# Expert weights relaid by partition, loaded in a half and two quarters (in) and in halves (out), with one quarter going through a buffer of its own

## The chip, the cores and the metric

The kernel runs on one core of one Trainium2 chip. The metric is device time in microseconds (us) of that core, for one launch. The comparisons are between medians of runs on the same chip.

## The reference, cut to what matters

Two transformer blocks on 256 tokens of width 1024, all in float32. The first block (gated attention and retention mixer, convolutional feed-forward) and the mixer of the second block come first; the end of the second block is a mixture of 32 experts, and that is where the change is:

```python
logits = (t @ w_router + b_router)            # 256 tokens, 32 experts
top_val, top_idx = lax.top_k(logits, 4)       # each token goes to 4 experts
gate_w = jax.nn.softmax(top_val, axis=-1)
...
hb = xb @ w_exp_in[e] + b_exp_in[e]           # xb: the tokens of expert e; w_exp_in[e]: 1024 x 2048
g = jnp.minimum(hb[:, :1024], 7.0)
u = jnp.clip(hb[:, 1024:], -7.0, 7.0)
a = g * jax.nn.sigmoid(1.702 * g) * (u + 1.0)
y = a @ w_exp_out[e] + b_exp_out[e]           # w_exp_out[e]: 1024 x 1024
...
h = layer_norm(ALPHA * h + sum over the 4 experts of gate_w * y)
```

One expert has 8 MB of in-weights and 4 MB of out-weights, read once: 32 experts are about 403 MB (12.58 million bytes each), out of 494 MB that the whole kernel moves.

## The kernel before, in words

**Tiling of an expert.** The contraction over 1024 goes in 8 steps k of 128 rows. `win` holds the in-weights of one expert (8 steps of 128 x 2048), `wout` its out-weights (8 steps of 128 x 1024). Both lie in `big_mem` and there is one of each: a step's place is free for the next expert once TensorE has used it. The tokens of an expert are gathered by matmuls with a 0/1 matrix (`gather`, L1038) into `xT`. They are worked in groups of 32, 64, or 64 and 32 rows, by how many tokens the expert has (`GROUPS`); an expert with more than 64 tokens has two groups, 96 rows together.

**One expert on TensorE** (`one_pass`): `gu` (L1055) adds up 8 steps of in-weights, counting `gu_part` after each step; then gathers for the next expert, transposes for the way back (L1077) and of the activations (L1085); then `second` (L1097) adds up 8 steps of out-weights, counting `y_part`; then `combine` (L1111, L1120) adds the result to the tokens' rows in PSUM, and the next expert's `gu` begins. VectorE (L2320 to L2332) and ScalarE (L1706, L1713, L1717, L1722) do the activation and the copies out of PSUM between these.

**The loads** are all issued by SyncE (SP) onto one queue, in program order. Before: four quarters of `win` (2 MB each, two steps) and four of `wout` (1 MB each). Each DMA waits until TensorE has used the two steps it overwrites, and SP goes through its waits in order. TensorE waits for a quarter before the first step that it covers. In DRAM the rows are taken so that partition p has rows 2p and 2p+1 of a 256-row piece; so the gather and the transpose take every second column (a stride of 2 in `h1` and `moe["a"]`).

**Order.** Experts 0 and 1 come first, then the others in an order that VectorE works out from the token counts (`order`, L2352), which spaces the large ones out.

**Before the experts** the DMA queue carries the dense weights through a ring of three slots (`load`, L393), each load waiting for its slot. The in-weights of expert 0 are issued at L460, its out-weights at L463, those of the later experts at L477 and L480.

Of the kernel before, what the change touches and what calls it, by code (L numbers as in the profile page):

```python
# [7 lines left out]
F32 = mybir.dt.float32  # L8
# [5 lines left out]
ACT = mybir.ActivationFunctionType  # L14
# [89 lines left out]
x0_in x1_in tab_stay_in tab1_in cols_in small_in router_in tab2_in rows_in rows_out toep_in toep_ps toep_ready ln12_in bias_in  # L104
slot0_in slot1_in slot2_in up0_in up1_in
own_act own_dve square_ready root_ready
# [17 lines left out]
def program(nc, ins, out):  # L124
# [3 lines left out]
    with ExitStack() as ctx:  # L128
        s = {n: ctx.enter_context(nc.semaphore(n)) for n in EVENTS}
        win_in = [ctx.enter_context(nc.semaphore(f"win{k}_in")) for k in range(KD // 2)]  # L130
        wout_in = [ctx.enter_context(nc.semaphore(f"wout{k}_in")) for k in range(KD // 2)]


        ring_mem = ctx.enter_context(nc.sbuf_tensor("ring_mem", [P, 3 * 4096], F32))
# [248 lines left out]
        wout_x = ins["w_exp_out_2"].rearrange("l e (k p j) n -> (l e) k p j n", p=P, j=2)  # L383


        @block.sync
        def _(sp):
# [70 lines left out]
            sp.wait_ge(s["merged_ready"], KD)  # L458
            for k in range(KD // 2):
                sp.dma_start(win[:, 2 * k:2 * k + 2, :], win_x[0, k]).then_inc(win_in[k], 16)  # L460
            sp.wait_ge(s["out_ps"], T)
            for k in range(KD // 2):
                sp.dma_start(wout[:, 2 * k:2 * k + 2, :], wout_x[0, k]).then_inc(wout_in[k], 16)  # L463

            sp.wait_ge(s["counts_ready"], 1)
            done = sp.alloc_register("sp_done")
            sp.reg_mov(done, 0)

            def expert(before, cur):
# [5 lines left out]
                for k in range(KD // 2):  # L475
                    sp.wait_ge(s["gu_part"], KD * others + 2 + 2 * k)
                    sp.dma_start(win[:, 2 * k:2 * k + 2, :], win_x[cur, k]).then_inc(win_in[k], 16)  # L477
                for k in range(KD // 2):
                    sp.wait_ge(s["y_part"], KD * others + 2 + 2 * k)
                    sp.dma_start(wout[:, 2 * k:2 * k + 2, :], wout_x[cur, k]).then_inc(wout_in[k], 16)  # L480

            expert(slice(0, 1), 1)
            sp.wait_ge(s["order_ready"], 1)
            with sp.Fori(2, E) as e:
                before = sp.value_load(order[0:1, bass.ds(e - 1, 1)], min_val=0, max_val=E - 1)
                expert(bass.ds(before, 1), sp.value_load(order[0:1, bass.ds(e, 1)], min_val=0, max_val=E - 1))
            for t in range(T):
# [61 lines left out]
        def _(pe):  # L549
# [483 lines left out]
            def gather(lo, hi, bank=7):  # L1033

                for k in range(lo, hi):
                    c = SLOTS * (k % EARLY)
                    for t in range(T):
                        last = mm(ps[:, bank, c:c + SLOTS], h1[:, t, SEQ * (k // 2) + k % 2:SEQ * (k // 2 + 1):2], moe["picks"][:, t, :], start=(t == 0), stop=(t == T - 1))  # L1038
                if hi in (EARLY, KD):
                    last.then_inc(s["gather_ps"], 1)  # L1040
# [6 lines left out]
            def gu(blocks, landed_all, tokens_all):  # L1047
# [15 lines left out]
                for k in range(KD):  # L1063
                    if k == EARLY:
                        pe.wait_ge(s["xT_ready"], tokens_all)
                    if k % 2 == 0:
                        pe.wait_ge(win_in[k // 2], landed_all)
# [12 lines left out]
            def turn_a(at, m):  # L1080

                w = D * m // P
                for c in range(w // P):
                    place = ps[:, 5, P * c:P * (c + 1)] if m > XS else ps[:, 4 + at // XS, SEQ + P * c:SEQ + P * (c + 1)]
                    last = nc.tensor.transpose(place, moe["a"][:, KD * at + SEQ * (c // 2) + c % 2:KD * at + SEQ * (c // 2 + 1):2], ident)  # L1085
                last.then_inc(s["aT_ps"], 1)

            def second(blocks, landed_all):

                for k in range(KD):  # L1090
                    if k % 2 == 0:
                        pe.wait_ge(wout_in[k // 2], landed_all)
                    for b, (at, m) in in_turn(blocks, k):
# [33 lines left out]
            for t in range(T):  # L1127
                if t == 0:
                    pe.wait_ge(s["pick0_ready"], 1)
                else:  # L1130
                    pe.wait_ge(s["picks_ready"], 1)
                    pe.wait_ge(s["h1_ready"], T)
                for k in range(KD):
                    c = SLOTS * (k % EARLY)
                    last = mm(ps[:, 7 if k < EARLY else 6, c:c + SLOTS], h1[:, t, SEQ * (k // 2) + k % 2:SEQ * (k // 2 + 1):2], moe["picks"][:, t, :],
                              start=(t == 0 and k in (0, EARLY)), stop=(t == T - 1), skip_group_check=True)
                    if t == T - 1 and k in (EARLY - 1, KD - 1):
                        last.then_inc(s["gather_ps"], 1)
# [99 lines left out]
        def _(act):  # L1238
# [518 lines left out]
            with act.Fori(0, E) as e:  # L1757
# [5 lines left out]
                with act.If(extra > 0):  # L1763
                    with act.If(extra < 2):
                        one_pass(GROUPS[1])
                    with act.If(extra > 1):
# [4 lines left out]
                        act.nop()  # L1771
                    act.nop()
                act.nop()
                act.wait_ge(s["order_ready"], 1)
# [673 lines left out]
```

## Time and profile before

| | us |
|---|---|
| median of 3 runs (1468.63 to 1469.0) | 1468.64 |
| the profiled execution: its own time | 1468.93 |
| its span, first to last instruction | 1467.1 |
| TensorE busy (share of the span) | 1314.9 (90%) |
| VectorE busy | 464.9 (32%) |
| ScalarE busy | 390.4 (27%) |
| GpSimd busy | 221.7 (15%) |
| longest shares of the chain that ended last | DMA of in-weights 25%, TensorE L1055 16%, TensorE L1097 7% |

The page of the profile has the busy time of each engine, a strip of 40 slices over the span, the chain of waits that ended last, the costliest groups of instructions, and the DMA issues with the time until they landed. A matmul's busy time says when the array had work, not how well it was used. Where an engine was idle, the view names what ended the idle time. The experts take the last 25 of the 40 slices.

### The profile page before, as it was taken

What the parts mean: (1) busy time and instruction counts of PE and PEld (TensorE: products, weight loads), DVE (VectorE), ACT (ScalarE), POOL (GpSimd) and SP (SyncE); (2) the same over time, 40 slices, a digit from 0 to 9 for tenths busy, and PEclk for the clock granted to TensorE, in tenths of its full rate; (3) what the DMA queues carried; (4) which work ended last, traced back from release to release, by engine and by line L of the source; (5) the groups of instructions that cost most, each with busy time, mean ns of one, the idle gap of its engine ahead of it and who ended that gap; (6) DMA issues with size and microseconds to landing.
All of it is one profiled execution on the core that took longest, in us unless ns stands there. A gap on an engine that the chain in (4) does not pass through costs nothing.

```text
span 1467.1 us, 25925 instructions
## 1 busy us (share of the span) xinstructions
PE 1314.9 (90%) x9475; PEld 819.1 (56%) x9476; DVE 464.9 (32%) x916; ACT 390.4 (27%) x728; POOL 221.7 (15%) x129
## 2 busy tenths in 40 slices
PE   7999999999999997887899888988889988998886
PEld 7787999878999853343334433443433434343333
DVE  2756777664534961111102110211111101110112
ACT  5556666555657420000001000110010001000101
POOL 6772122007774300000000000000000000000000
PEclk9999999999999999999999999999999999999998
DMA  9432667755443789999999999999999999999996
GB/s 329 170 113 58 181 185 234 287 193 178 167 173 116 269 334 421 425 429 424 425 426 428 427 426 424 427 427 427 424 428 427 421 424 428 427 426 424 428 426 273
DMA packets 114537, 494.40 MB, mean 337 GB/s; under 512 B 7633, under 2 KB 57153, under 8 KB 81505
## 3 DMA queue, kind: packets, MB, share of 16 engines
q1 hardware_dynamic: 113011, 491.50, 83.4%
q10 hardware_dynamic: 1486, 2.34, 0.5%
q8 instruction: 28, 0.46, 0.1%
q14 instruction: 12, 0.10, 0.0%
HBM read 492.76 MB, written 1.06 MB: 337 GB/s over the span
## 4 chain that ended last, share of the span: by engine, by line
PE 59%; DMA 29%; DVE 5%; issue 3%; ACT 3%; POOL 1%; SPq 0%; DVEq 0%; ACTq 0%; POOLq 0%
DMA big_mem<-in_w_exp_in 25%; PE ps L1055 16%; PE ps L1097 7%; PE ps L579 6%; PE ps L581 5%; PE ps L580 5%; PE ps L1038 3%; DMA big_mem<-in_w_exp_out 3%; PE ps L797 1%; PE ps L799 1%; PE ps L798 1%; PE ps L1120 1%; PE ps L1111 1%; PE ps L1085 1%; PE ps L599 1%
## 5 line engine op out<-in xcount | busy, mean ns | idle before, releaser
L1055 PE MATMUL ps<-big_mem,ring_mem 128*32 128x512 f32 (+1 forms) x2304 | 370.5, 622 | 49.5 <-DMA big_mem<-in_w_exp_in 49.5
L1055 PEld LDWEIGHTS ps<-big_mem,ring_mem 128*32 128x32 f32 (+1 forms) x2304 | 111.8, 122 | 284.6 <-issue 197.6
L1097 PE MATMUL ps<-big_mem,x 128*32 128x256 f32 (+1 forms) x1888 | 186.3, 438 | 5.0 <-ACT x L1722 3.3
L579 PE MATMUL ps<-hT_hi,w_hi 128*128 128x256 f32 x600 | 171.3, 285 | 1.3 <-DVE hT_lo L1812 1.3
L580 PE MATMUL ps<-hT_lo,w_hi 128*128 128x256 f32 x600 | 169.7, 283 | 0.0
L581 PE MATMUL ps<-hT_hi,w_lo 128*128 128x256 f32 x600 | 169.7, 283 | 0.0
L1038 PEld LDWEIGHTS ps<-ring_mem,h 128*128 128x128 f32 x1024 | 132.9, 199 | 61.3 <-issue 61.3
L1038 PE MATMUL ps<-ring_mem,h 128*128 128x96 f32 x1024 | 150.2, 291 | 0.0
L2320 DVE TENSOR_SCALAR ring_mem<-ps 128x256 f32<-128x256 f32 (+1 forms) x36 | 18.7, 520 | 402.7 <-PE ps L1055 402.7
L1706 ACT ACTIVATE ring_mem<-ring_mem 128x256 f32<-128x256 f32 (+1 forms) x36 | 17.7, 493 | 465.1 <-DVE ring_mem L2320 465.1
L1097 PEld LDWEIGHTS ps<-big_mem,x 128*32 128x32 f32 (+1 forms) x1888 | 72.2, 117 | 105.4 <-issue 69.1
L1713 ACT ACTIVATE ring_mem<-ps 128x480 f32<-128x480 f32 x65 | 32.0, 493 | 349.2 <-PE ps L1038 342.4
L579 PEld LDWEIGHTS ps<-hT_hi,w_hi 128*128 128x128 f32 x600 | 115.0, 192 | 5.0 <-issue 3.1
L580 PEld LDWEIGHTS ps<-hT_lo,w_hi 128*128 128x128 f32 x600 | 115.1, 192 | 0.0
L581 PEld LDWEIGHTS ps<-hT_hi,w_lo 128*128 128x128 f32 x600 | 115.0, 192 | 0.0
L533 POOL TENSOR_TENSOR w_lo<-ring_mem,w_hi 128x1024 fp32r<-128x1024 f32 x38 | 92.2, 2437 | 111.1 <-DVE w_lo L2077 77.1
L2332 DVE COPY ring_mem<-ps 128x256 f32<-128x256 f32 (+1 forms) x36 | 18.4, 520 | 277.4 <-PE ps L1097 277.4
L2310 DVE TENSOR_SCALAR ring_mem<-stay,posb,gate 128x128 f32<-128x128 f32 x72 | 21.3, 344 | 106.7 <-PE ps L1038 88.3
L1055 PE MATMUL ps<-ring_mem 128*32 128x512 bf16 (+1 forms) x144 | 18.7, 426 | 31.1 <-ACT ring_mem L1713 16.4
L1438 ACT ACTIVATE w_hi<-ring_mem 128x1024 fp32r<-128x1024 f32 x44 | 44.9, 1051 | 0.1
L2038 DVE SCALAR_TENSOR_TENSOR big_mem<-ps,cols,big_mem 128x255 f32<-128x255 f32 (+1 forms) x88 | 38.4, 478 | 17.2 <-ACT big_mem L1476 13.0
L1528 ACT ACTIVATE w_hi<-ring_mem 128x1024 fp32r<-128x1024 f32 x39 | 41.0, 1054 | 10.2 <-PE ps L581 6.9
(430 smaller groups left out, 1719.7 us busy)
## 6 DMA issues: line engine op xcount, KB each, us to landing
big_mem<-in_w_exp_in SPq DMA_DIRECT2D x128, 2048.0 KB, 22.3
big_mem<-in_w_exp_out SPq DMA_DIRECT2D x128, 1024.0 KB, 21.3
ring_mem<-in_w_in SPq DMA_DIRECT2D x14, 2048.0 KB, 8.1
ring_mem<-in_w_up SPq DMA_DIRECT2D x44, 512.0 KB, 4.8
ring_mem<-in_w_down SPq DMA_DIRECT2D x5, 2048.0 KB, 11.3
ring_mem<-in_w_out SPq DMA_DIRECT2D x4, 2048.0 KB, 8.2
ring_mem<-in_w_branch_a SPq DMA_DIRECT2D x1, 2048.0 KB, 7.6
ring_mem<-in_w_branch_b SPq DMA_DIRECT2D x1, 2048.0 KB, 7.6
```

The lines of the kernel that those rows point to most:

```text
L533: nc.gpsimd.tensor_tensor(split_piece(w2_lo, p), piece(p), split_piece(w2_hi, p).bitcast(F32), ALU.subtract).then_inc(s["piece_lo"], 1)
L579: mm(out, hi, x_hi, start=start, stop=False)
L580: mm(out, hi, x_lo, start=False, stop=False)
L581: return mm(out, lo, x_hi, start=False, stop=stop)
L1038: last = mm(ps[:, bank, c:c + SLOTS], h1[:, t, SEQ * (k // 2) + k % 2:SEQ * (k // 2 + 1):2], moe["picks"][:, t, :], start=(t == 0), stop=( ...
L1055: last = mm(out, stationary, weights[:, f, w * q:w * (q + 1)] if m > XS else weights[:, :, w * q:w * (q + 1)], start=start, stop=stop)
L1097: last = mm(ps[m * q:m * (q + 1), 4 + at // XS, 0:w], aT[:, k % n, k // n, :], wout[:, k, w * q:w * (q + 1)], start=(k == 0), stop=(k == K ...
L1438: run(quarter(w_hi, b), up_slot[u][:, :, g, :], ACT.Copy).then_inc(s[f"hi{b}"], 1)
L1528: run(split_piece(w2_hi, p), piece(p), ACT.Copy).then_inc(s["piece_hi"], 1)
L1713: run(moe["xT"][:, lo:hi, :].rearrange("p k m -> p (k m)"), src, ACT.Copy).then_inc(s["xT_ready"], 1)
L2038: last = v.scalar_tensor_tensor(c, ps[:, 4 + u, SEQ * g:SEQ * (g + 1) - i], cols[:, bass.ds(tap + f, 1)], c, ALU.mult, ALU.add)
L2310: last = v.tensor_scalar(moe["source"][:, b, P * t:P * (t + 1)].rearrange("p (z m) -> p z m", m=m), copies, where(t, e, p), gate[:, t, bas ...
```

## The change

- The host hands over `w_exp_in` and `w_exp_out` with each expert as [128 partitions][8 steps][row]: partition p has the rows 128k + p for all k, one after the other, 64 KB of in-weights and 32 KB of out-weights. A step k is then the plain block of 128 rows, and the gather and the transpose take 128 neighbouring columns.
- In-weights come in three parts: steps 0 to 3 (4 MB, 32 KB in one run per partition), steps 4 and 5 (2 MB), steps 6 and 7 (2 MB). Out-weights come in two halves of 2 MB, 16 KB in one run per partition.
- Steps 6 and 7 of the next expert go to `ahead`, a new buffer of 2 MB. ScalarE copies them into `win` (two copies of 128x2048) at the end of its work for the present expert, and TensorE waits for these copies before step 6. For expert 0 they are loaded straight into `win`; for expert 1 the load into `ahead` is issued before the two loads of `w_branch`.
- SP issues for each expert, in this order: the quarter into `ahead` (after ScalarE's copies have emptied it), the half and the quarter of `win`, the two halves of `wout`. A part is issued when TensorE has used all the steps that it overwrites.

```diff
+WIN_PARTS = ((0, 4), (4, 6), (6, 8))
+WOUT_PARTS = ((0, 4), (4, 8))
...
-        win_x = ins["w_exp_in_2"].rearrange("l e (k p j) n -> (l e) k p j n", p=P, j=2)
+        win_x, wout_x = ins["w_exp_in_2"], ins["w_exp_out_2"]
...
+            sp.dma_start(ahead[:], win_x[1, :, WIN_PARTS[-1][0]:WIN_PARTS[-1][1], :]).then_inc(s["ahead_in"], 16)
             load(25, w_rows("w_branch_a_2", 0, 4))
...
-                for k in range(KD // 2):
-                    sp.wait_ge(s["gu_part"], KD * others + 2 + 2 * k)
-                    sp.dma_start(win[:, 2 * k:2 * k + 2, :], win_x[cur, k]).then_inc(win_in[k], 16)
-                for k in range(KD // 2):
-                    sp.wait_ge(s["y_part"], KD * others + 2 + 2 * k)
-                    sp.dma_start(wout[:, 2 * k:2 * k + 2, :], wout_x[cur, k]).then_inc(wout_in[k], 16)
+                for n, (a, b) in enumerate(WIN_PARTS[:-1]):
+                    sp.wait_ge(s["gu_part"], KD * others + b)
+                    if a == 0:
+                        sp.sem_inc(s["refill_due"], 1)
+                    sp.dma_start(win[:, a:b, :], one(win_x, cur, a, b)).then_inc(win_in[n], 16)
+                for n, (a, b) in enumerate(WOUT_PARTS):
+                    sp.wait_ge(s["y_part"], KD * others + b)
+                    if a == 0:
+                        sp.sem_inc(s["refill_due"], 1)
+                    sp.dma_start(wout[:, a:b, :], one(wout_x, cur, a, b)).then_inc(wout_in[n], 16)
...
+                cur = sp.value_load(order[0:1, bass.ds(e, 1)], min_val=0, max_val=E - 1)
+                sp.wait_ge(win_in[-1], 16 * e)
+                sp.sem_inc(s["refill_due"], 1)
+                sp.dma_start(ahead[:], one(win_x, cur, *WIN_PARTS[-1])).then_inc(s["ahead_in"], 16)
+                expert(bass.ds(before, 1), cur)
...
-                        last = mm(ps[:, bank, c:c + SLOTS], h1[:, t, SEQ * (k // 2) + k % 2:SEQ * (k // 2 + 1):2], moe["picks"][:, t, :], ...)
+                        last = mm(ps[:, bank, c:c + SLOTS], h1[:, t, P * k:P * (k + 1)], moe["picks"][:, t, :], ...)
...
+                with act.If(e < E - 1):
+                    act.wait_ge(s["ahead_in"], 16 * e + 16)
+                    for z, k in enumerate(range(*WIN_PARTS[-1])):
+                        last = run(win[:, k, :], ahead[:, z, :], ACT.Copy)
+                    last.then_inc(win_in[-1], 16)
```

SyncE, the body of the loop over the experts, before: each DMA with the wait ahead of it (`gu_part`, `y_part` count TensorE's used steps).

```order
L477 ISA [waits gu_part]
L477 DMA big_mem<-in_w_exp_in 128x4096
L476 REGISTER_ALU
L477 ISA [waits gu_part]
L477 DMA big_mem<-in_w_exp_in 128x4096
...
L480 ISA [waits y_part]
L480 DMA big_mem<-in_w_exp_out 128x2048
L480 ISA [waits y_part]
L480 DMA big_mem<-in_w_exp_out 128x2048
```

The same place now: `win2_in` is the semaphore that ScalarE's copies count.

```order
L501 ISA [waits win2_in]
L501 DMA ahead<-in_w_exp_in 128x4096
...
L487 REGISTER_ALU [waits gu_part]
L487 DMA big_mem<-in_w_exp_in 128x8192
L484 REGISTER_ALU
L487 ISA [waits gu_part]
L487 DMA big_mem<-in_w_exp_in 128x4096
L492 ISA [waits y_part]
L492 DMA big_mem<-in_w_exp_out 128x4096
L489 REGISTER_ALU
L492 ISA [waits y_part]
L492 DMA big_mem<-in_w_exp_out 128x4096
```

Eight DMAs with eight waits became five with five. The quarter for steps 6 and 7 has moved from fourth place to the front, ahead of steps 0 to 3, and stands behind the last wait on `y_part` of the expert before.

ScalarE, the end of its body for one expert, before: the copy of the activations for `second` (L1722), then the number of the next expert.

```order
L1722 ACTIVATE x<-ps 128x512 [waits aT_ps]
L1722 ACTIVATE x<-ps 128x256 [waits aT_ps]
...
L1775 ISA [waits order_ready]
L1775 TENSOR_LOAD order
```

The same place now:

```order
L1740 ACTIVATE x<-ps 128x512 [waits aT_ps]
L1740 ACTIVATE x<-ps 128x256 [waits aT_ps]
...
L1795 ACTIVATE big_mem<-ahead 128x2048 [waits ahead_in]
L1795 ACTIVATE big_mem<-ahead 128x2048
...
L1799 ISA [waits order_ready]
L1799 TENSOR_LOAD order
```

Two copies of 128x2048 stand between the activations' copy of one expert and the first work for the next.

## Rows read from the trace of the kernel before

**Rows 1.** Stretches: us; busy us of each engine (instructions); granted clock, DMA share, GB/s.
```profile
529.00:534.00 5.00, 4.67 (x24) 2.12 (x26) 4.79 (x7) 1.44 (x2) 0.00 (x0) 1.00 0.00 0
700.00:800.00 100.00, 90.86 (x654) 38.68 (x654) 14.40 (x37) 8.21 (x18) 0.00 (x0) 1.00 1.01 426
```

**Rows 2.** In-weight loads: us from issue to landing, least, median, most.
```profile
DMA to landing us min/median/max: 7.5/22.3/27.4
```

**Rows 3.** TensorE, four in-weight quarters waited for: start us, us, [idle before].
```profile
640.83 3.71 PE L1055 MATMUL ps<-big_mem,ring_mem 128*64 128x512 f32 x16 [1.19 <-DMA big_mem<-in_w_exp_in]
645.73 3.70 PE L1055 MATMUL ps<-big_mem,ring_mem 128*64 128x512 f32 x16 [1.19 <-DMA big_mem<-in_w_exp_in]
734.29 1.92 PE L1055 MATMUL ps<-big_mem,ring_mem 128*32 128x512 f32 x16 [2.87 <-DMA big_mem<-in_w_exp_in]
1442.89 3.25 PE L1055 MATMUL ps<-big_mem,ring_mem 128*32 128x512 f32 x16 [2.63 <-DMA big_mem<-in_w_exp_in]
```

**Rows 4.** SyncE, two loads of dense weights before the experts.
```profile
417.95 0.37 SPq L393 DMA_DIRECT2D ring_mem<-in_w_in  x1
431.27 0.37 SPq L393 DMA_DIRECT2D ring_mem<-in_w_branch_a  x1
```

**Rows 5.** TensorE and SyncE around expert 0 (64 rows), timeline.
```profile
529.81 13.95 PE L1055 MATMUL ps<-big_mem,ring_mem 128*64 128x512 f32 x64
533.49 10.63 SPq L477 DMA_DIRECT2D big_mem<-in_w_exp_in  x4
549.24 7.09 PE L1097 MATMUL ps<-big_mem,x 128*64 128x512 f32 x32 [0.24 <-ACT x L1722]
```

**Rows 6.** How many groups the 32 experts have (one copy L2332 each).
```profile
L2332 DVE COPY ring_mem<-ps x36: 414/425/693, 556.4 to 1455.1; 128x256 f32<-128x256 f32 x23, 128x512 f32<-128x512 f32 x13
```

**Rows 7.** Timeline around an expert of 96 rows, from the last out-weights before it.
```profile
744.22 1.07 PE L1097 MATMUL ps<-big_mem,x 128*32 128x256 f32 x16 [0.17 <-DMA big_mem<-in_w_exp_out]
...
749.41 0.98 PE L1055 MATMUL ps<-ring_mem 128*64 128x512 bf16 x8 [1.34 <-ACT ring_mem L1713]
750.23 22.12 PE L1055 MATMUL ps<-big_mem,ring_mem 128*32 128x512 f32 x128
...
778.44 11.68 PE L1097 MATMUL ps<-big_mem,x 128*32 128x256 f32 x96 [0.28 <-ACT x L1722]
...
781.71 8.94 SPq L480 DMA_DIRECT2D big_mem<-in_w_exp_out  x4
```

**Rows 8.** TensorE's clock after it stood idle (columns as in Rows 1).
```profile
578.00:585.00 7.00, 0.52 (x4) 0.35 (x3) 0.96 (x4) 0.41 (x1) 0.00 (x0) 0.63 0.98 415
585.00:588.00 3.00, 2.82 (x16) 0.73 (x20) 0.00 (x0) 0.00 (x0) 0.00 (x0) 0.50 1.02 418
588.00:591.00 3.00, 3.00 (x24) 0.81 (x20) 0.00 (x0) 0.00 (x0) 0.00 (x0) 0.66 1.02 426
```

**Rows 9.** The end of the queue (columns as in Rows 1), and TensorE's last out-weights.
```profile
1451.00:1452.00 1.00, 0.97 (x16) 0.63 (x18) 0.00 (x0) 0.36 (x2) 0.00 (x0) 1.00 0.63 262
...
1451.41 3.66 PE L1097 MATMUL ps<-big_mem,x 128*32 128x256 f32 x64
```

**Rows 10.** TensorE, an expert of 64 rows and the next one's start, and one of 32.
```profile
695.91 13.95 PE L1055 MATMUL ps<-big_mem,ring_mem 128*64 128x512 f32 x64
...
715.34 7.09 PE L1097 MATMUL ps<-big_mem,x 128*64 128x512 f32 x32 [0.24 <-ACT x L1722]
...
725.87 0.41 PE L1055 MATMUL ps<-ring_mem 128*32 128x512 bf16 x4
...
795.42 7.05 PE L1055 MATMUL ps<-big_mem,ring_mem 128*32 128x512 f32 x64
...
807.47 3.66 PE L1097 MATMUL ps<-big_mem,x 128*32 128x256 f32 x64
```

**Rows 11.** A ScalarE copy of 1024 columns (ns least, median, most).
```profile
L1352 ACT ACTIVATE w_bc<-ring_mem x10: 1041/1058/1064, 9.5 to 106.5; 128x1024 fp32r<-128x1024 f32 x10
```

**Rows 12.** DMA issues on the page: KB each, median us to landing.
```profile
ring_mem<-in_w_in SPq DMA_DIRECT2D x14, 2048.0 KB, 8.1
```

More of the change, by code:

```diff
@@ L129, in program @@
         s = {n: ctx.enter_context(nc.semaphore(n)) for n in EVENTS}
-        win_in = [ctx.enter_context(nc.semaphore(f"win{k}_in")) for k in range(KD // 2)]
-        wout_in = [ctx.enter_context(nc.semaphore(f"wout{k}_in")) for k in range(KD // 2)]
+        win_in = [ctx.enter_context(nc.semaphore(f"win{n}_in")) for n in range(len(WIN_PARTS))]
+        wout_in = [ctx.enter_context(nc.semaphore(f"wout{n}_in")) for n in range(len(WOUT_PARTS))]
+        ahead = ctx.enter_context(nc.sbuf_tensor("ahead", [P, 2, 2 * FE], F32))
         ring_mem = ctx.enter_context(nc.sbuf_tensor("ring_mem", [P, 3 * 4096], F32))
@@ L458, in _ @@
             sp.wait_ge(s["merged_ready"], KD)
-            for k in range(KD // 2):
-                sp.dma_start(win[:, 2 * k:2 * k + 2, :], win_x[0, k]).then_inc(win_in[k], 16)
+            for n, (a, b) in enumerate(WIN_PARTS):
+                sp.dma_start(win[:, a:b, :], win_x[0, :, a:b, :]).then_inc(win_in[n], 16)
             sp.wait_ge(s["out_ps"], T)
-            for k in range(KD // 2):
-                sp.dma_start(wout[:, 2 * k:2 * k + 2, :], wout_x[0, k]).then_inc(wout_in[k], 16)
+            for n, (a, b) in enumerate(WOUT_PARTS):
+                sp.dma_start(wout[:, a:b, :], wout_x[0, :, a:b, :]).then_inc(wout_in[n], 16)
             sp.wait_ge(s["counts_ready"], 1)
@@ L467, in _, with one @@
             sp.reg_mov(done, 0)
+            def one(weights, cur, a, b):
+                if isinstance(cur, int):
+                    return weights[cur, :, a:b, :]
+                return weights[bass.ds(cur, 1), :, a:b, :].rearrange("e p k n -> p (e k) n")
             def expert(before, cur):
@@ L474, in expert @@
                 sp.reg_add(done, done, 1)
[L475 to L480 removed]
+                for n, (a, b) in enumerate(WIN_PARTS[:-1]):
[3 more added lines that the diff above has]
+                    sp.dma_start(win[:, a:b, :], one(win_x, cur, a, b)).then_inc(win_in[n], 16)
+                for n, (a, b) in enumerate(WOUT_PARTS):
+                    sp.wait_ge(s["y_part"], KD * others + b)
+                    if a == 0:
+                        sp.sem_inc(s["refill_due"], 1)
+                    sp.dma_start(wout[:, a:b, :], one(wout_x, cur, a, b)).then_inc(wout_in[n], 16)
             expert(slice(0, 1), 1)
@@ L1037, in gather @@
                     for t in range(T):
-                        last = mm(ps[:, bank, c:c + SLOTS], h1[:, t, SEQ * (k // 2) + k % 2:SEQ * (k // 2 + 1):2], moe["picks"][:, t, :], start=(t == 0), stop=(t == T - 1))
+                        last = mm(ps[:, bank, c:c + SLOTS], h1[:, t, P * k:P * (k + 1)], moe["picks"][:, t, :], start=(t == 0), stop=(t == T - 1))
                 if hi in (EARLY, KD):
@@ L1065, in gu @@
                         pe.wait_ge(s["xT_ready"], tokens_all)
-                    if k % 2 == 0:
-                        pe.wait_ge(win_in[k // 2], landed_all)
+                    for n, (a, _) in enumerate(WIN_PARTS):
+                        if k == a:
+                            pe.wait_ge(win_in[n], landed_all)
                     for b, (at, m) in in_turn(blocks, k):
@@ L1084, in turn_a @@
                     place = ps[:, 5, P * c:P * (c + 1)] if m > XS else ps[:, 4 + at // XS, SEQ + P * c:SEQ + P * (c + 1)]
-                    last = nc.tensor.transpose(place, moe["a"][:, KD * at + SEQ * (c // 2) + c % 2:KD * at + SEQ * (c // 2 + 1):2], ident)
+                    last = nc.tensor.transpose(place, moe["a"][:, KD * at + P * c:KD * at + P * (c + 1)], ident)
                 last.then_inc(s["aT_ps"], 1)
@@ L1090, in second @@
                 for k in range(KD):
-                    if k % 2 == 0:
-                        pe.wait_ge(wout_in[k // 2], landed_all)
+                    for n, (a, _) in enumerate(WOUT_PARTS):
+                        if k == a:
+                            pe.wait_ge(wout_in[n], landed_all)
                     for b, (at, m) in in_turn(blocks, k):
@@ L1134, in _ @@
                     c = SLOTS * (k % EARLY)
-                    last = mm(ps[:, 7 if k < EARLY else 6, c:c + SLOTS], h1[:, t, SEQ * (k // 2) + k % 2:SEQ * (k // 2 + 1):2], moe["picks"][:, t, :],
+                    last = mm(ps[:, 7 if k < EARLY else 6, c:c + SLOTS], h1[:, t, P * k:P * (k + 1)], moe["picks"][:, t, :],
                               start=(t == 0 and k in (0, EARLY)), stop=(t == T - 1), skip_group_check=True)
@@ L2436 @@
     from concourse.bass_utils import run_bass_kernel_spmd
-    nc = bacc.Bacc("TRN2", target_bir_lowering=False, num_devices=1)
+    nc = bacc.Bacc("TRN2", target_bir_lowering=False, num_devices=1, dynamic_dma_scratch_size=128)
     arrays, ins = {}, {}
     given = {n: np.ascontiguousarray(inputs[n]) for n in _INS}
+    for n in ("w_exp_in_2", "w_exp_out_2"):
+        a = np.asarray(inputs[n])[0]
+        given[n] = np.ascontiguousarray(a.reshape(E, KD, P, a.shape[-1]).transpose(0, 2, 1, 3))
     for name, a in list(given.items()) + list(tables().items()):
```

5 lines of the change are left out of this document (2 added, 3 removed).

## The prediction, made before the changed kernel was run

> **What bounds the kernel now.** I read the strip of stretches first. From about 534 us to the end the DMA engines have a share of 1.01 and move 426 GB/s, in every stretch alike [rows 1]; TensorE is at 91% there, but that is matmuls in flight. So in the experts' stage the DMA queue is the bound. Then the time to landing: the least is 7.5 us for a quarter of 2 MB, the median 22.3 [rows 2], so some four transfers stand in the queue when one is issued. Last, where TensorE waits: most waits are for in-weights. Two neighbouring quarters land 645.73 - 640.83 = 4.90 us apart, and the fourth quarters of two experts that are 24 apart land 1442.89 - 734.29 = 708.6 us apart, 29.53 per expert [rows 3]. Four in-quarters are 19.6 of it, which leaves 9.93 for the out-weights, 2.48 for each quarter of 1 MB. The only hole in the queue lies before the stage: 0 GB/s from 529 to 534 [rows 1], while expert 1 waits for expert 0's first two steps.
>
> A gain must therefore come from faster transfers, fewer bytes inside the stage, or an earlier start; and any stop of the queue is paid in full. What kept the queue full was its reserve, and the question is whether the new order keeps it.
>
> **The change, part by part.** The sum is made against the profiled execution (1468.93 us; span 1467.1), 0.3 above the median of the runs.
>
> 1. Longer runs, fewer DMAs. Two transfers of 1 MB take 4.96 us, one of 2 MB takes 4.90: 0.065 less for one merge that doubles the run of a partition. Each expert has three merges (two in the out-weights, one in the in-weights): 3 x 0.065 x 31 = -6.0 us. The trace has no run of 32 KB; the bounds are 0 and, since both figures are rounded, 0.1 per merge, -9.3. The sum takes -6.0.
>
> 2. Expert 1's last quarter is loaded before the stage. It is issued behind the load at 417.95, and the next load comes only at 431.27 [rows 4]. Two transfers of 4.9 and 2.6 around them end by 430.4: nothing is pushed back. The stage has one quarter less: -4.9.
>
> 3. The first release is later. Before, the queue restarts at 533.49, when expert 0 (64 rows) has done two steps; a step is 13.95/8 = 1.74 [rows 5]. Now four steps are needed: +3.5, to 537.0.
>
> 4. A first hole. From 537.0 + 0.7 the queue has a half and a quarter, 14.7, till 552.4. The first half of `wout` is free when `second` has done four of eight steps, 549.24 + 7.09/2 = 552.8 [rows 5], and SyncE and the issue take 0.9 (of the 2.8 in item 5): 553.7. +1.3.
>
> 5. The experts of 96 rows. 36 groups in 32 experts make four with two groups [rows 6]. Before one of them the last out-weights landed at 744.22, and its `gu` began at 750.23, just when its first in-quarter could be there (744.2 + 4.9 = 749.1) [rows 7]. Now the queue brings first the quarter for steps 6 and 7, which TensorE wants last, and then a half: steps 0 to 3 are there 14.7 after the out-weights. By items 1 to 4 the queue is some 1.5 us earlier by then, so TensorE is ready near 749.5 and gets its half near 757: about 7 us idle. From that landing both sides run a race to the first half of the next `wout`:
>  - TensorE: from `gu`'s start to `second`'s is 778.44 - 750.23 = 28.2; four of its steps 11.68/2 = 5.8, SyncE 0.2 [rows 7]; issue and landing cost 7.5 - 4.9 = 2.6 beyond the transfer [rows 2]. Together 36.8.
>  - The queue: what stands between is a quarter, two halves of `wout`, the quarter for `ahead`, a half and a quarter: 7 x 4.9 = 34.3, less 0.1. 34.2.
>  The queue runs dry for 2.6 us. The second half of `wout` is released 5.8 later, after a transfer of 4.9: 0.9 more. The next quarter for `ahead` can't fill the hole, though ScalarE has emptied that buffer: SyncE is behind its wait on `y_part`. Before, the same count from the first quarter had 44 us of transfers ahead of it and released after two steps, so there was a reserve of about 10. 4 x (2.6 + 0.9) = +14.0. No row shows the race itself; its bounds are 0 (the reserve holds) and, with 1 us more on TensorE's side for waits that I have not seen, +18. Experts of 64 rows have the same 34.2 against 13.95 + 5.5 + 3.5 + 2.8 = 25.8 [rows 10], and don't stop the queue.
>
> 6. The clock. After an idle stretch of 6 us the granted clock was 0.50 for 3 us and 0.66 for the next three [rows 8], where full is 2.4 GHz and half 1.2: 1.5 + 1.0 = 2.5 us lost. A quarter waited for 2.63 took 3.25 where one after 2.87 took 1.92 [rows 3]: 1.3 lost, or nothing. An idle stretch of 7 us ahead of each large expert puts this on the losing side of the race. Bounds 0 and 3; I take 2.0, as 7 us is nearer to the first case: 4 x 2.0 = +8.0.
>
> 7. ScalarE's two copies are 128x2048 each, 2 x 2 x 1.06 = 4.2 us at most [rows 11]. They start when `second` does and TensorE needs them at step 6 of the next `gu`; in the shortest expert `second`, `combine` and six steps are over 12 us. Cost nothing; without that cover it would be up to 4.2 x 31.
>
> 8. Gather and transpose with neighbouring columns: off the bound, nothing; they could give the race some tenths, below or above.
>
> 9. The tail. Before, the queue ended near 1451.6 and `second` at 1455.1: 3.5 later [rows 9]. Now, from the landing of the half of expert 30 (64 rows), TensorE needs 715.34 + 7.09 - 695.91 = 26.5, then 3.7 to the first step, then 807.47 + 3.66 - 795.42 = 15.7 [rows 10], 45.9; the queue ends 34.2 + 9.8 - 1.9 = 42.1 after it (1.9: what a landing lags behind the transfer, the 2.6 of item 5 without the issue). 3.8, so +0.3, and +2.0 for the clock, as TensorE waits there too: +2.3.
>
> Sum: -6.0 - 4.9 + 3.5 + 1.3 + 14.0 + 8.0 + 2.3 = +18.2: 1487.1 profiled, 1487 in the median.
>
> **A rule that speaks against the layout.** The pieces of neighbouring partitions lay 16 KB apart in DRAM and now lie 64 KB apart. The trace has no transfer with this pitch. The nearest is `w_in`, short runs at a wide pitch: 8.1 us to landing [rows 12] against 7.5 for the contiguous quarter, so between 0 and 0.6 per quarter of 2 MB. As most of that is the short runs, the forecast takes 0. The Trainium skill ("DMA: Bandwidth & Descriptors", Latency and other measured facts) says that row pitches at large powers of two slow HBM copies: 207 GB/s each way at 512 KiB against 214 at full rate, and far less at megabytes. By it a pitch of 64 KB would cost little, and by its 3% the stage of some 917 us would take about 28 us more.
>
> **The rivals.**
> - Full clock. TensorE's idle stretches are cut short (by the gathers, or since ScalarE's copies and tokens arrive otherwise), and the clock stays at full. For it: 2.87 us of waiting left it full [rows 3]. Against: 7 us. Then 8.0 and 2.0 fall out: 1477.
> - No dry queue, and so faster. If the path from the landing of the half to the release of `wout` is under 34.2 us, or TensorE gets the half sooner, the reserve holds, and what is left is -6.0 - 4.9 + 3.5 + 1.3 + 0.3 = -5.8: 1463 (1459 with the full gain of item 1). It decides at 34.2. For it: before, the queue never ran dry after 534. Against: 36.8 is summed from single rows, and I'd have to be 2.6 out.
> - The layout doesn't stream: the pitch slows HBM, or runs of 32 KB are cut up so that nothing is saved. Priced at 0.05 per 2 MB, 6 x 0.05 x 31 = 9, on top of the forecast and without item 1's 6.0: 1500. For it nothing in the trace; no row excludes it.
> - The waits on `ahead`: ScalarE comes late and TensorE waits at step 6. Up to 4.2 for some experts; it only counts on the four large ones, +5 to +17 beyond the forecast: 1498. Against: the quarter is first in the queue.
>
> **How the numbers follow.** Forecast 0.50; full clock 0.23; no dry queue 0.15; layout 0.06; late copies 0.06. What a measurement of this kernel can tell from no change is about 0.2%, 2.9 us. Faster comes from the third case, with a sliver of it within 2.9 us, and the low edge of the full-clock case adds as much to no change: faster 0.14, same 0.04, slower 0.82. The forecast's own range is 1480 to 1492, a clock loss of 0.6 to 3 in the five places. The range goes from 1464, which takes in the upper part of the third case, to 1496.
>
> **What would show it.** In the strip, the DMA share falls below 1 near 552 and four times, near 790, 942, 1152 and 1305, for 3 to 6 us and again for 1, each time followed by an out-weight load landing in about 7.5 us. Waits of TensorE for in-weights become fewer and longer (about 7 us, ahead of the experts of 64 and 96 rows), with the granted clock at 0.5 behind them. Between the holes an expert takes about 29.3 us instead of 29.53. ScalarE's two copies end before `combine` does. If the DMA share stays at 1 through those four places, item 5 is wrong and the kernel is faster; if the holes are there with a clock of 1.00, item 6 is; if an expert takes over 29.6 between holes, item 1 is.

## The result, and the profile after

The changed kernel takes 1482.54 us in the median (1482.0 to 1482.87, 4 runs), the kernel before 1468.64 beside it (1467.24 to 1469.0). The ratio is 1.0096, 95% interval 1.0084 to 1.0107: 14 us slower. Its profiled execution has a span of 1480.2 us, 13.1 more than before.

Stretches of the changed kernel (columns as in Rows 1), the first four before and between the first experts and in the middle of the stage, then the four places where the prediction wants holes:

```profile
529.00:534.00 5.00, 4.99 (x26) 2.32 (x28) 4.86 (x6) 1.11 (x2) 0.00 (x0) 1.00 0.01 3
534.00:537.00 3.00, 3.00 (x16) 1.25 (x14) 1.34 (x3) 0.00 (x0) 0.00 (x0) 1.00 0.00 0
552.00:554.00 2.00, 2.00 (x12) 0.60 (x10) 0.00 (x0) 0.37 (x1) 0.00 (x0) 1.00 0.87 246
820.00:930.00 110.00, 91.05 (x662) 38.75 (x662) 12.54 (x37) 18.13 (x22) 0.00 (x0) 0.92 1.01 433
785.00:790.00 5.00, 4.68 (x41) 1.70 (x41) 0.00 (x0) 4.38 (x4) 0.00 (x0) 1.00 0.61 262
790.00:795.00 5.00, 5.00 (x48) 1.50 (x44) 0.00 (x0) 0.07 (x1) 0.00 (x0) 1.00 0.43 131
940.00:945.00 5.00, 5.00 (x44) 1.56 (x44) 0.00 (x0) 0.81 (x1) 0.00 (x0) 1.00 0.28 62
1150.00:1155.00 5.00, 5.00 (x44) 1.49 (x36) 0.00 (x0) 1.36 (x1) 0.00 (x0) 1.00 0.23 49
1300.00:1305.00 5.00, 5.00 (x46) 1.52 (x44) 0.00 (x0) 2.63 (x2) 0.00 (x0) 1.00 0.27 115
```

Before, the DMA share was 1.01 from 534 us to the end [rows 1]. Now the queue starts 3.2 us later (SyncE issues at 536.68, before at 533.49) and runs out once ahead of each large expert's next `wout`. In between it is quicker than before, 433 GB/s against 426. No packet moves for 3.85, 3.28, 4.24 and 3.23 us at the four places, by the packets' records in the trace. The same records give the time from one expert's worth of bytes (12.58 million) to the next, the "period" below: away from the holes it is 29.13 us, before 29.51. The four experts with a hole take 35.37, 34.30, 35.55 and 34.66 us, 23.4 more in all than four plain ones.

The timeline of the changed kernel around the first of them, TensorE, ScalarE and SyncE (it answers [rows 7]):

```profile
742.16 3.66 PE L1115 MATMUL ps<-big_mem,x 128*32 128x256 f32 x64
745.82 3.71 ACT L1795 ACTIVATE big_mem<-ahead 128x2048 f32<-128x2048 f32 x2 [3.71 <-DMA ahead<-in_w_exp_in]
749.99 1.61 PE L1071 MATMUL ps<-ring_mem 128*64 128x512 bf16 x8 [1.41 <-ACT ring_mem L1731]
755.53 24.27 PE L1071 MATMUL ps<-big_mem,ring_mem 128*32 128x512 f32 x128 [3.93 <-DMA big_mem<-in_w_exp_in]
769.08 5.76 SPq L487 DMA_DIRECT2D big_mem<-in_w_exp_in  x2
785.78 11.68 PE L1115 MATMUL ps<-big_mem,x 128*32 128x256 f32 x96 [0.32 <-ACT x L1740]
791.99 6.00 SPq L492 DMA_DIRECT2D big_mem<-in_w_exp_out  x2
799.89 0.34 SPq L501 DMA_DIRECT2D ahead<-in_w_exp_in  x1
```

TensorE's bias matmuls at 749.99 take 1.61 us (0.98 in [rows 7]), then it waits 3.93 us for the half. Then `gu` takes 24.27 us where it took 22.12. From its start to the start of `second` there are 30.25 us (before 28.2), the first out-half is issued at 791.99, and the queue has been empty since about 789. ScalarE's copies (3.71 us for both) end long before step 6. At the other three large experts the wait is 5.03, 6.10 and 4.98 us. The granted clock in the first wait and behind it (same columns):

```profile
750.00:756.00 6.00, 2.07 (x12) 0.49 (x16) 1.48 (x6) 0.00 (x0) 0.00 (x0) 0.50 1.00 429
758.00:760.00 2.00, 2.00 (x8) 0.52 (x5) 0.00 (x0) 0.00 (x0) 0.00 (x0) 0.52 1.07 459
760.00:762.00 2.00, 2.00 (x12) 0.69 (x8) 0.00 (x0) 0.00 (x0) 0.00 (x0) 1.00 0.97 418
```

The clock is at half (1.2 GHz) from the bias matmuls on, and for the first 4.4 us of `gu`: 2.2 us lost there. At the other three it covers the first 3.3, 5.3 and 3.3 us of `gu` (the trace's clock records), 8 us lost in all.

The page of the changed kernel: the strip, the costliest wait of TensorE, ScalarE's copies, the issues (KB each, median us to landing).

```profile
GB/s 342 160 105 67 188 185 239 259 213 195 140 214 115 329 277 428 436 428 428 432 438 359 427 432 432 370 432 431 432 434 430 355 432 437 428 367 431 432 437 246
...
L1071 PE MATMUL ps<-big_mem,ring_mem 128*32 128x512 f32 (+1 forms) x2304 | 374.2, 626 | 64.4 <-DMA big_mem<-in_w_exp_in 64.4
...
L1795 ACT ACTIVATE big_mem<-ahead 128x2048 f32<-128x2048 f32 x62 | 114.9, 1902 | 53.8 <-DMA ahead<-in_w_exp_in 51.2
...
big_mem<-in_w_exp_in SPq DMA_DIRECT2D x32, 4096.0 KB, 18.9
big_mem<-in_w_exp_out SPq DMA_DIRECT2D x64, 2048.0 KB, 15.3
big_mem<-in_w_exp_in SPq DMA_DIRECT2D x33, 2048.0 KB, 20.8
ahead<-in_w_exp_in SPq DMA_DIRECT2D x31, 2048.0 KB, 18.4
```

Four slices of the strip fall to 355 to 370. A transfer now lands sooner after its issue than before [rows 2], though the queue is no quicker to that degree: it is shorter when the transfer is issued. That is the lost reserve.

### The profile page after: what moved, and what is told of

Its sections match the earlier page's. It is cut to its first block, busy times and chain, and to the rows that moved or that the text cites. A ratio compares the mean times of both kernels' runs of the same rounds, so it can differ in the third digit from the quotient of the medians.

```text
span 1480.2 us, 25865 instructions
## 1 busy us (share of the span) xinstructions
PE 1308.4 (88%) x9475; PEld 815.4 (55%) x9476; DVE 464.9 (31%) x916; ACT 503.5 (34%) x790; POOL 221.6 (15%) x129
## 4 chain that ended last, share of the span: by engine, by line
PE 69%; DMA 17%; DVE 5%; issue 4%; ACT 4%; POOL 1%; ACTq 0%; DVEq 0%; SPq 0%; POOLq 0%
PE ps L1071 23%; DMA big_mem<-in_w_exp_in 17%; PE ps L1115 10%; PE ps L595 6%; PE ps L597 5%; PE ps L596 5%; PE ps L1054 4%; PE ps L1129 2%; PE ps L813 1%; PE ps L815 1%; PE ps L814 1%; PE ps L1138 1%; PE ps L1102 1%; ACT x L1740 1%; PE ps L615 1%
## 5 line engine op out<-in xcount | busy, mean ns | idle before, releaser
L1071 PE MATMUL ps<-big_mem,ring_mem 128*32 128x512 f32 (+1 forms) x2304 | 374.2, 626 | 64.4 <-DMA big_mem<-in_w_exp_in 64.4
L1071 PEld LDWEIGHTS ps<-big_mem,ring_mem 128*32 128x32 f32 (+1 forms) x2304 | 118.6, 125 | 301.7 <-issue 229.1
L1054 PEld LDWEIGHTS ps<-ring_mem,h 128*128 128x128 f32 x1024 | 124.0, 191 | 57.8 <-issue 57.8
L1054 PE MATMUL ps<-ring_mem,h 128*128 128x96 f32 x1024 | 141.6, 281 | 0.0
L1795 ACT ACTIVATE big_mem<-ahead 128x2048 f32<-128x2048 f32 x62 | 114.9, 1902 | 53.8 <-DMA ahead<-in_w_exp_in 51.2
L2356 DVE COPY ring_mem<-ps 128x256 f32<-128x256 f32 (+1 forms) x36 | 18.4, 520 | 269.8 <-PE ps L1115 269.8
## 6 DMA issues: line engine op xcount, KB each, us to landing
ahead<-in_w_exp_in SPq DMA_DIRECT2D x31, 2048.0 KB, 18.4
```

The lines of the kernel that those rows point to most:

```text
L1054: last = mm(ps[:, bank, c:c + SLOTS], h1[:, t, P * k:P * (k + 1)], moe["picks"][:, t, :], start=(t == 0), stop=(t == T - 1))
L1071: last = mm(out, stationary, weights[:, f, w * q:w * (q + 1)] if m > XS else weights[:, :, w * q:w * (q + 1)], start=start, stop=stop)
L1795: last = run(win[:, k, :], ahead[:, z, :], ACT.Copy)
```

## The experiments

Each was timed beside the kernel before, in 4 to 11 runs, and each ratio is to the kernel before of the same session. "Layout" is the new order of the weights in DRAM; every kernel with it also has the changed kernel's place of the buffers in SBUF.

**layout_only.** Both weights in quarters, no buffer of its own:

```diff
-WIN_PARTS = ((0, 4), (4, 6), (6, 8))
-WOUT_PARTS = ((0, 4), (4, 8))
+WIN_PARTS = WOUT_PARTS = ((0, 2), (2, 4), (4, 6), (6, 8))
-                sp.dma_start(ahead[:], one(win_x, cur, *WIN_PARTS[-1])).then_inc(s["ahead_in"], 16)
-                with act.If(e < E - 1):   # and ScalarE's copies
```

> The new layout of the weights alone: four quarters of in-weights and four of out-weights as in the kernel before, no buffer of its own. Theory (the loss is the queue running dry before the four experts of 96 rows): no holes and transfers as before, so 1468 to 1469 us. Rival (the pitch of 64 KB slows the stream): above 1471. Rival (the layout itself is what makes an expert's transfers take 29.13 us instead of 29.5): 31 x 0.38 = 12 less, about 1457.

1459.64 us, ratio 0.9943 (0.9931 to 0.9955), no hole, period 29.26. My theory had 1468 to 1469; what came is nearest to the last rival, without showing that it is the layout. Nothing is merged here, and yet two thirds of the gain in the period are there. The prediction has no term for that.

**out_halves.** The same with `WOUT_PARTS = ((0, 4), (4, 8))`.

> The new layout with in-weights in four quarters, out-weights in halves, no buffer of its own. The first in-quarter is again first in the queue, and it is released after two steps: 44 us of transfers ahead of a path of about 37 (39 with the slow clock). Theory: no holes; the merges of the out-weights save 2 x 0.065 to 2 x 0.14 per expert: 4 to 9 us, so 1460 to 1465, if merges are what shortens an expert. Rival (halves of out-weights are released too late and themselves empty the queue): four holes of 1 to 3 us and 1465 to 1475.

1459.89 us, 0.9935 (0.9922 to 0.9948); period 29.17, with small stops at the large experts. Two merges bring 0.09 us per expert, and coarser releases take it back.

**quarters_ahead.** The changed kernel with the first four steps in two quarters: `WIN_PARTS = ((0, 2), (2, 4), (4, 6), (6, 8))`.

> The changed kernel with the half of in-weights cut into two quarters (0 to 1, 2 to 3, 4 to 5, and 6 to 7 through the buffer of its own, which still comes first). The first steps are there 4.9 us sooner, so the queue has 39 us against a path of 37 to 39. Theory: the four holes vanish or shrink below 1 us each, one hole of about 5 us stays at expert 1's out-weights (only three quarters are queued there): about 1460, up to 1465. Rival (the buffer of its own, ScalarE's copies or SyncE's wait on them cause the loss): the holes stay, 1475 to 1483.

1463.31 us, 0.9965 (0.9952 to 0.9978). The four places cost 0.6, 1.1, 2.0 and 0 us in place of 5.2 to 6.4, and at expert 1's out-weights the queue is empty for 2.2 us. Against out_halves the buffer, its copies and the preloaded quarter together cost 3.4 us, and one cut, the half, the other 19.

**warm96.** The changed kernel with the bias matmuls of the 96-row experts done five times over, ahead of the wait for the half (the four extra rounds are added up and then overwritten by the one that starts the sum anew):

```diff
+                for _ in range(4 if len(blocks) > 1 else 0):
+                    for at, m in blocks:
+                        each(at, m, own[:, 0:m], bias_gu, True, True)
                 for at, m in blocks:
                     each(at, m, own[:, 0:m], bias_gu, True, False)
```

> The changed kernel, with the bias matmuls of the four experts of 96 rows repeated five times, so that TensorE works about 4 us longer while it waits for its half. Theory (the slow clock behind the idle stretch costs about 2 us on the path to the release in each): granted clock at full there, holes shorter by about 2 us each, 1482.5 - 8 = 1474 to 1476. Rival (the path is bound by the steps and waits alone, the clock is no part): 1482 to 1483 or, if the repeats delay the steps, above.

1475.49 us, 1.0045 (1.0031 to 1.0059): 7 us less than the changed kernel for more work on TensorE. Its timeline at the same expert:

```profile
750.50 4.63 PE L1071 MATMUL ps<-ring_mem 128*64 128x512 bf16 x40 [1.43 <-ACT ring_mem L1734]
755.81 22.16 PE L1071 MATMUL ps<-big_mem,ring_mem 128*32 128x512 f32 x128 [0.68 <-DMA big_mem<-in_w_exp_in]
783.96 11.68 PE L1118 MATMUL ps<-big_mem,x 128*32 128x256 f32 x96 [0.32 <-ACT x L1743]
790.17 6.00 SPq L492 DMA_DIRECT2D big_mem<-in_w_exp_out  x2
```

`gu` starts with the landing as before, takes 22.16 and not 24.27, and the first out-half is issued 1.8 us sooner. The holes shrink to 1.71, 1.73, 3.34 and 1.72 us. The third place is the exception: there the extra rounds did not keep the clock up.

```profile
1113.25 23.83 PE L1071 MATMUL ps<-big_mem,ring_mem 128*32 128x512 f32 x128 [2.64 <-DMA big_mem<-in_w_exp_in]
```

```profile
1111.50:1114.60 3.10, 1.35 (x10) 0.36 (x12) 0.00 (x0) 0.00 (x0) 0.00 (x0) 1.00 0.82 349
1114.60:1118.00 3.40, 3.40 (x10) 1.04 (x8) 0.00 (x0) 0.00 (x0) 0.00 (x0) 0.50 0.95 405
```

So the slow clock was a cause of its own: where it is gone the hole is 1.5 to 2.1 us shorter, where it stayed only 0.9. At full clock there are still holes.

**half_no_ahead.** The changed kernel's parts, all three straight to `win` (the loads into `ahead` and the copies are left out as in layout_only).

> The changed kernel without the buffer of its own: the in-weights in a half and two quarters, all straight to win, the out-weights in halves. The reserve theory: the first transfer of an expert is now the half that TensorE wants first, but its release still waits for four steps. Ahead of the four experts with two groups the queue runs dry once, by less than in the changed kernel, for some 2 to 3 us each, and expert 1 begins 3.5 us later; with the period of 29.2, the sum is between -2 and +4 against before: 1466 to 1472 us, about 10 under the changed kernel. The theory that the coarse first half alone makes the holes, whichever transfer is first, says the same four holes of 3.2 to 4.2 us and a time no more than 5 us (the preloaded quarter) from the changed kernel's 1482.5. The theory that only the buffer makes them says no hole and 1463 us (quarters' 1459.9 plus the later first release).

1478.32 us, 1.0067 (1.0053 to 1.0081): 18.4 over out_halves, from which it differs only in the half. I had given it 6 to 12 less. The stretches at the first large expert:

```profile
800.00:802.00 2.00, 1.82 (x20) 0.64 (x24) 0.95 (x4) 0.36 (x1) 0.00 (x0) 1.00 0.87 369
802.00:804.00 2.00, 2.00 (x24) 0.62 (x20) 0.00 (x0) 0.00 (x0) 0.00 (x0) 1.00 0.06 25
804.00:806.00 2.00, 2.00 (x26) 0.50 (x17) 0.00 (x0) 0.00 (x0) 0.00 (x0) 1.00 0.97 270
806.00:808.00 2.00, 2.00 (x21) 0.86 (x14) 0.47 (x2) 0.01 (x1) 0.00 (x0) 1.00 0.61 262
```

and its timeline:

```profile
752.77 24.65 PE L1067 MATMUL ps<-big_mem,ring_mem 128*32 128x512 f32 x128 [2.59 <-DMA big_mem<-in_w_exp_in]
...
789.61 6.00 SPq L491 DMA_DIRECT2D big_mem<-in_w_exp_out  x2
...
804.29 3.70 SPq L486 DMA_DIRECT2D big_mem<-in_w_exp_in  x3
```

TensorE has its half 2.8 us sooner than in the changed kernel, but the next half is released only at 804.29, when four steps of the next `gu` are done, and the hole stands there. It also waits long enough for the slow clock (24.65), which my figure left out. Of the three cases, the coarse first half has the time nearest (4 us from the changed kernel), and the reserve theory missed by 6 us. So the half makes the holes with or without the buffer; the buffer's place in the order moves them from the in-weights to the out-weights.

**ahead_last.** The load into `ahead` stands behind the other in-weights:

```diff
                 for n, (a, b) in enumerate(WIN_PARTS[:-1]):
                     ...
+                if refill is not None:
+                    sp.wait_ge(win_in[-1], 16 * refill)
+                    sp.dma_start(ahead[:], one(win_x, cur, *WIN_PARTS[-1])).then_inc(s["ahead_in"], 16)
```

> The changed kernel with one thing moved: the load of the next expert's last quarter stands behind the in-weights' other two parts in SyncE's order, not ahead of them. The same transfers, releases, copies and the same preloaded quarter. The reserve theory: what comes first is now the half that TensorE waits for, so it gets it 4.9 us sooner, while the release at step 4 stays: holes of 1 to 3 us ahead of the four large experts, idle times of TensorE short enough for the clock to stay at full at some of them, 1470 to 1478 us. If the order of the two does nothing (the holes come from the coarse release alone), the holes stay at 3.2 to 4.2 us and the time at 1482 us. If the copies come too late in this order, TensorE waits at step 6 of most experts and the time goes past 1485 us.

1487.83 us, 1.0130 (1.0115 to 1.0146), the slowest of all: the third of the cases in its time, late copies, though the wait is at another step than I said. The timeline one expert earlier, and two groups of the page:

```profile
733.47 4.47 PE L1072 MATMUL ps<-big_mem,ring_mem 128*32 128x512 f32 x40
735.62 3.71 ACT L1796 ACTIVATE big_mem<-ahead 128x2048 f32<-128x2048 f32 x2 [12.94 <-DMA ahead<-in_w_exp_in]
737.35 3.93 SPq L487 DMA_DIRECT2D big_mem<-in_w_exp_in  x2
739.24 0.39 ACT L1732 ACTIVATE ring_mem<-ps 128x288 f32 x1
739.68 2.78 PE L1072 MATMUL ps<-big_mem,ring_mem 128*32 128x512 f32 x24 [1.74 <-ACT ring_mem L1732]
```

```profile
L1072 PE MATMUL ps<-big_mem,ring_mem 128*32 128x512 f32 (+1 forms) x2304 | 380.6, 642 | 67.9 <-ACT ring_mem L1732 66.9
...
L1796 ACT ACTIVATE big_mem<-ahead 128x2048 f32<-128x2048 f32 x62 | 115.0, 1902 | 421.4 <-DMA ahead<-in_w_exp_in 421.4
```

TensorE stops after 40 of 64 matmuls, five of the eight steps. What it waits for is not the copied weights but the rest of the expert's tokens (L1732, 128x288), which ScalarE copies out of PSUM only behind its two copies of weights; those had waited 12.94 us for the load. Of 68 us waited for at this line, 66.9 are ended by L1732. The load stood first in the changed kernel for a reason: there the copies wait 51.2 us in all, against 421.4, and all of TensorE's 64.4 us at this line are ended by in-weights' DMAs.

**before_shifted.** What made the period shorter without a merge? The changed kernel also makes the scratch for dynamic DMAs smaller (`dynamic_dma_scratch_size=128`), which "The change" doesn't say. The new buffer takes 16,384 bytes of each partition, the smaller scratch gives 16,256 back, and so all buffers behind them lie 128 bytes further on. The kernel before, with the changed kernel's place in SBUF alone:

```diff
+        ahead = ctx.enter_context(nc.sbuf_tensor("ahead", [P, 2, 2 * FE], F32))   # unused
         ring_mem = ctx.enter_context(nc.sbuf_tensor("ring_mem", [P, 3 * 4096], F32))
-    nc = bacc.Bacc("TRN2", target_bir_lowering=False, num_devices=1)
+    nc = bacc.Bacc("TRN2", target_bir_lowering=False, num_devices=1, dynamic_dma_scratch_size=128)
```

> The kernel before, with its own layout, transfers and order, but with the buffer of 16 KB per partition that the change adds allocated (and never used) in front of the same buffers, and with the same small scratch for dynamic DMAs, so that win, wout and the rest lie at the addresses they have in the changed kernel. The layout-only kernel was 0.9943 of before, with a period of 29.26 us per expert instead of 29.51. If the layout in DRAM brings that, this kernel stays at 1468 us (ratio 0.998 to 1.002) with a period of 29.5. If the place of the buffers in SBUF brings it, this kernel goes to 1460 us (ratio 0.994) with a period of 29.26. I give the layout 0.75.

1460.73 us, 0.9943 (0.9929 to 0.9956), period 29.26. The layout, to which I had given 0.75, is not needed for it: layout_only has the same period.

**pitch16.** layout_only with each quarter as one contiguous block in DRAM: `.reshape(E, P, KD // 2, 2, n).transpose(0, 2, 1, 3, 4)` behind the new order.

> As the layout-only kernel (row k*128+p of a weight at partition p, quarters, no ahead), but each quarter lies in DRAM as one contiguous block: the pieces of neighbouring partitions are 16 KB apart (8 KB for the out-weights) as before, not 64 KB (32 KB). If the pitch across partitions is what made the transfers quicker, this goes back to 1468 us and a period of 29.5. If the pitch does nothing and the gain of 0.25 us per expert has come from elsewhere (the other addresses in SBUF, or gather and transpose with neighbouring columns), it stays at 1460 us and 29.26. I give the pitch 0.65, on the ground that layout-only changed nothing else in a transfer.

1459.84 us, 0.9939 (0.9925 to 0.9953), period 29.26. A pitch of 16 or of 64 KB across partitions is the same here; I had given the pitch 0.65.

**shift128.** The kernel before and 128 unused bytes per partition: `nc.sbuf_tensor("ahead", [P, 32], F32)` ahead of `ring_mem`, nothing else.

> The kernel before with one unused buffer of 128 bytes per partition allocated ahead of the rest, nothing else: win moves from byte 65,536 of each partition to 65,664, wout from 131,072 to 131,200. That is where they lie in the changed kernel. If the address of the weights in SBUF made the transfers quicker, this kernel has the period of 29.26 us per expert and 1460 us (ratio 0.994). If the smaller scratch for dynamic DMAs did it, it stays at 1468 to 1469 us and 29.51. I give the address 0.7.

**scratch_only.** The small scratch, and `[P, 4064]` in front, so that all addresses are as before.

> The kernel before with the small scratch for dynamic DMAs of the changed kernel, and an unused buffer of 16,256 bytes per partition in front that keeps every address as it was (win at 65,536). If the scratch's size made the transfers quicker: 1460 us, 29.26 us per expert. If the address did, nothing changes: 1468 to 1469 us, 29.51. If both are needed together, neither this nor the kernel with the shift alone is faster.

**down2048.** The same with `[P, 3552]`.

> As the one before, but the unused buffer is 2048 bytes shorter, so that win lies at byte 63,488 and wout at 129,024: off the powers of two, but still on multiples of 2048. If only the small scratch counts, 1460 us. If the address counts and any place off the multiple of 65,536 does, 1460 us too, with the scratch alone at 1468. If it takes a place off the multiples of 2048, 1468 us. No theory of mine chooses between the last two.

shift128: 1461.19 us, 0.9949 (0.9935 to 0.9963), period 29.26. scratch_only: 1468.95, 1.0002 (0.9993 to 1.0011), 29.51. down2048: 1468.24, 1.0000 (0.9991 to 1.0009), 29.51. The row of 820 to 930 us in each (columns as in Rows 1), of the kernel before:

```profile
820.00:930.00 110.00, 92.69 (x652) 41.09 (x648) 15.51 (x41) 9.97 (x22) 0.00 (x0) 0.97 1.01 426
```

and of shift128:

```profile
820.00:930.00 110.00, 95.11 (x678) 41.85 (x672) 15.52 (x41) 9.96 (x22) 0.00 (x0) 0.97 1.01 430
```

It is the address of the buffers: 128 bytes up is enough, 2048 bytes down does nothing, and nor does the smaller scratch alone.

**preload_qqh.** Layout, in-weights in quarters, out-weights in two quarters and a half; only expert 1's last quarter goes through `ahead` (`act.If(e < 1)`).

> The parts that paid, together: new layout and addresses, in-weights in quarters straight to win, out-weights in two quarters and a half, and expert 1's last quarter alone loaded before the stage and copied by ScalarE; no later expert uses the buffer. By the reserve theory nothing is released later than before, so no hole at the four large experts. Against the layout-only kernel (1459.6): the preloaded quarter saves 4.9 us, of which 2.9 come back as a hole before expert 1's first out-quarter (three quarters from 534.3 end at 549.0; two steps of second are done at 551.0, issued 551.9), the out half saves 0.05 x 31 = 1.5 us: 1456 us, between 1454 and 1459, the fastest so far. If the holes of the changed kernel come from the buffer and not from the half, the four holes stay and it is over 1470 us.

1459.43 us, 0.9935 (0.9922 to 0.9949): beats both kernels, by 0.6% and 1.6%, but not layout_only, and misses the 1454 to 1459 that I had expected. Its four large experts have no hole, and the period is 29.22. The 4.9 us of the quarter are lost at expert 1:

```profile
549.00:552.00 3.00, 3.00 (x8) 0.73 (x6) 0.00 (x0) 3.00 (x2) 0.00 (x0) 0.50 0.04 11
552.00:557.00 5.00, 5.00 (x26) 1.67 (x22) 0.00 (x0) 0.35 (x1) 0.00 (x0) 0.96 0.74 265
```

From about 549.7 all but one of the DMA engines are idle, and then all, until TensorE's first steps of `second` are done and SyncE issues at 552.37. This stretch is TensorE's, so a transfer taken out of it buys nothing. The clock is at half there in the traces of layout_only, out_halves, warm96 and pitch16 too, and at full in those of before, after, before_shifted and quarters_ahead. Why, no run shows.

## Why the prediction was right

The forecast was +18.2 us, the profiled executions differ by 13.1.

- **Item 1 is the term that was mis-sized.** It gave -6.0 to longer runs; transfers gained 0.38 x 31 = 11.8. Of these, merging gave 0.09 (out_halves) + 0.04 (the half: 29.13) = 0.13 per expert, 4.0 us, a third less than forecast. The other 7.8 come from an effect that the working doesn't name: the new buffer moves `win` and `wout` by 128 bytes. That one term makes up more than the whole 5 us between forecast and result.
- **Items 2 to 4.** First release +3.2 (forecast +3.5). From its start to its end the queue took 925.1 us, before 917.8. Of these 7.3, 23.4 stand at the large experts, -11.8 are item 1, -4.9 is the quarter less, and 0.6 are left for the first hole (forecast 1.3).
- **Items 5 and 6**, the heart of it: forecast 14.0 + 8.0 = 22.0, measured 23.4, in four holes near 790, 942, 1152 and 1304 us. The race was read rightly at the first place: `gu` begins at 755.53, 36.5 later the half is issued, where 36.8 less 2.6 for issue and landing, and 2.0 for the slow clock on top, make 36.2. There the clock costs 30.25 - 28.15 = 2.1 us (changed kernel against warm96; forecast 2.0). Kept at full at three of the four places, it gives back 7.1 us in the median. The ground for the 2.0 was wrong, though, and that it fits is in part luck: I expected TensorE to idle 7 us before `gu`, and it idled 3.93, 5.03, 6.10 and 4.98. At three of the four places the clock had fallen before that wait began (899.9 and 1261.7 us by the clock records, as at 749.7).
- **Item 7.** The copies take 3.71 us a pair and hold up nobody in the changed kernel. ahead_last shows what happens without the cover: the tokens that stand behind the copies come late.
- **Item 9.** From the last packet (1462.75) to the end of `second` (1468.2) it is 5.4 us; before, 2.8 (1452.28 to 1455.07). That is +2.7 (forecast +2.3). The prediction's 3.5 for before took the queue's end as 1451.6, 0.7 too early by the packets' records. The clock loss that it forecast is there, at expert 30, after a wait of 6.70 us (13.95 in [rows 10]):

```profile
1419.43 17.02 PE L1071 MATMUL ps<-big_mem,ring_mem 128*64 128x512 f32 x64 [6.70 <-DMA big_mem<-in_w_exp_in]
```

Together: -11.8 - 4.9 + 3.2 + 0.6 + 23.4 + 2.7 = +13.2, against 13.1 measured.

Of the rivals, "full clock" falls with the rows at 0.50, "no dry queue" with the four holes; what it describes (1463) is how quarters_ahead came out (1463.31), whose first release comes two steps sooner. "The layout doesn't stream" falls with layout_only and pitch16 (by its own terms, 9 and 6 on top of 1487, its price was 1502, not the 1500 given). The rule on row pitches at large powers of two (the Trainium skill, "DMA: Bandwidth & Descriptors", Latency and other measured facts) starts its own figures at 512 KiB; these runs show that here 64 KB costs nothing that can be measured against 16 KB.

What isn't settled: why the two addresses tried that are multiples of 2048 are slower than the one 128 bytes on. With the kernel before, `win` lies at byte 65,536 of a partition and `wout` at 131,072. No run tried another odd place, or moved `win` and `wout` alone.

## What to carry to other kernels

In a stage that the queue bounds, a larger transfer is paid with a later release: here a half in place of two quarters won 0.04 us per expert and lost 18 us in all, though the reserve ran out only at the four largest of 32 experts. Size parts by the worst tile, and count the reserve there: transfers queued behind the landing against TensorE's path to the next release. And before a new layout gets the credit for a gain (or an added buffer the blame for a loss), run the old kernel with the new addresses; it is an edit of a line or two.

## What the hardware showed that I had not expected

- With the SBUF buffers 128 bytes further on, the transfers of the expert weights into them were quicker: mean time of a packet of 8 KB 313.5 ns before, scratch_only and down2048 too, 309.0 in shift128, before_shifted and pitch16; of 16 KB 615.4 against 612 (packets' records, 620 to 1400 us). It is 0.8% of the stage, 8 us of the kernel. The Trainium skill says, of reads, that a descriptor's transactions must start at multiples of 256 bytes, and that one which starts between them also pays for the bytes from the multiple below ("DMA: Bandwidth & Descriptors", How a descriptor splits into AXI transactions). If that held for the place written to as well, the shift should cost; here it gains.
- Merged transfers gained little once queued: 1213 ns in the median for a packet of 32 KB against two of 611. The changed kernel's 433 GB/s are next to the 435 that the Trainium skill gives as the ceiling of the fabric ("DMA: Bandwidth & Descriptors", Where 436 GB/s comes from). By that figure, as an estimate, the 426 of the kernel before had 2% left to win; no run here shows the ceiling itself.
- The clock can fall before the wait that I blamed: in the changed kernel it is at half in the bias matmuls at 749.99, ahead of the 3.93 us of waiting. In half_no_ahead a wait of 2.59 us was followed by half clock, while before, 2.87 us behind f32 matmuls left it at full [rows 3]. The length of the wait alone doesn't tell.
